# Gate rows of the expert blocks made on GpSimd instead of VectorE, in a two-layer diffusion step

## The reference

```python
    a = jax.nn.silu(hg) * hu * combine[..., None]
    y = jnp.einsum('nef,efd->nd', a, p["w_down"])
    ...
    x = x + g2 * _hier_moe(h2, p)      # once for the context, once for the latents
```

## Time and profile before

| | |
|---|---|
| time, median of 3 runs | 1197.59 us (1192.82 to 1198.98) |
| profiled execution: its own time, its span | 1193.6 us, 1191.8 us |
| TensorE clock granted, mean | 0.969 |
| busy: PE, DVE, ACT, POOL | 1068.1, 678.8, 433.7, 196.3 us |
| chain of waits: PE, DMA, DVE, POOL | 71%, 11%, 9%, 2% |
| mean DMA rate over the span | 224 GB/s |

### The profile page before, as it was taken

The page is one execution under the profiler, slowest core; times in us unless marked ns, Lnnn a source line. Parts: engine busy times, 40 slices in busy tenths (PEclk is TensorE's granted clock), DMA queues, the critical chain, the costliest instruction groups (busy, mean ns, idle before and its releaser), DMA issues.

```text
span 1191.8 us, 23434 instructions
## 1 busy us (share of the span) xinstructions
PE 1068.1 (90%) x9769; PEld 886.1 (74%) x9769; DVE 678.8 (57%) x1441; ACT 433.7 (36%) x935; POOL 196.3 (16%) x228
## 2 busy tenths in 40 slices
PE   3889999999999989999669999999999998999960
PEld 1567778889997668888447677888998876888850
DVE  1434466555466667766563336555446766666663
ACT  2332235652433413323242223655233342333321
POOL 0011140000021122221131112200001212222113
PEclk9999999999999999999889999999999999999985
DMA  9797989223337599999857998322243566999934
GB/s 316 238 242 206 230 276 348 71 77 107 107 105 261 199 350 360 371 359 379 286 180 213 240 232 251 94 71 71 76 141 102 213 226 220 339 363 372 378 114 176
DMA packets 136734, 267.00 MB, mean 224 GB/s; under 512 B 9989, under 2 KB 92069, under 8 KB 128432
## 3 DMA queue, kind: packets, MB, share of 16 engines
q1 hardware_dynamic: 118992, 219.13, 53.5%
q0 software_dynamic: 17024, 44.69, 13.3%
q10 hardware_dynamic: 608, 1.62, 0.4%
HBM read 248.71 MB, written 28.31 MB: 232 GB/s over the span
## 4 chain that ended last, share of the span: by engine, by line
PE 71%; DMA 11%; DVE 9%; issue 3%; ACT 3%; POOL 2%; SPq 1%; DVEq 0%; POOLq 0%; ACTq 0%
PE ps L938 16%; PE ps L809 16%; PE ps L1146 10%; PE ps L1058 6%; DMA ring<-in_w_down 5%; PE ps L1187 5%; PE ps L1073 5%; PE ps L690 3%; DMA ring<-in_ada_w 2%; DMA ring<-in_w_in 2%; PE ps L882 2%; PE ps L922 2%; PE ps L904 2%; PE ps L1136 1%; DMA arena<-scratch_xs,token_i 1%
## 5 line engine op out<-in xcount | busy, mean ns | idle before, releaser
L579 DVE TENSOR_TENSOR w_lo<-ring,w_hi 128x512 fp32r<-128x512 f32 x128 | 87.7, 690 | 162.1 <-ACT w_hi L568 162.0
L568 ACT ACTIVATE w_hi<-ring 128x512 fp32r<-128x512 f32 x128 | 80.3, 631 | 239.0 <-PE ps L809 142.0
L576 DVE TENSOR_TENSOR w_lo<-ring,w_hi 128x512 fp32r<-128x512 f32 x128 | 88.0, 689 | 109.9 <-ACT w_hi L566 109.9
L938 PE MATMUL ps<-h_hi,w_hi 128*128 128x384 f32 x384 | 133.8, 348 | 4.6 <-ACT arena L2175 4.6
L566 ACT ACTIVATE w_hi<-ring 128x512 fp32r<-128x512 f32 x128 | 80.4, 629 | 149.2 <-PE ps L938 103.8
L938 PE MATMUL ps<-h_hi,w_lo 128*128 128x384 f32 x384 | 128.8, 335 | 0.0
L938 PE MATMUL ps<-h_lo,w_hi 128*128 128x384 f32 x384 | 128.7, 335 | 0.0
L809 PE MATMUL ps<-w_hi,h_hi 128*128 128x512 f32 x288 | 117.0, 406 | 12.4 <-DVE w_lo L579 5.8
L809 PE MATMUL ps<-w_hi,h_lo 128*128 128x512 f32 x288 | 114.1, 396 | 0.0
L809 PE MATMUL ps<-w_lo,h_hi 128*128 128x512 f32 x288 | 114.1, 396 | 0.0
L1146 PEld LDWEIGHTS ps<-arena,ring 128*64 128x64 f32 x1920 | 80.2, 137 | 6.4 <-issue 6.3
(11 more groups left out here) (316 smaller groups left out, 2119.6 us busy)
## 6 DMA issues: line engine op xcount, KB each, us to landing
ring<-in_w_in SPq DMA_DIRECT2D x48, 1024.0 KB, 5.3
ring<-in_ada_w SPq DMA_DIRECT2D x44, 1024.0 KB, 10.2
ring<-in_w_down SPq DMA_DIRECT2D x18, 1024.0 KB, 17.0
ring<-in_w_up SPq DMA_DIRECT2D x16, 1024.0 KB, 13.2
ring<-in_w_gate SPq DMA_DIRECT2D x14, 1024.0 KB, 13.2
arena<-in_w_gate SPq DMA_DIRECT2D x10, 1024.0 KB, 9.2
scratch_ys<-x POOLq DMA_DIRECT2D x1, 9216.0 KB, 29.2
ring<-in_w_out SPq DMA_DIRECT2D x8, 1024.0 KB, 5.0
```

Source lines behind the costliest of these rows:

```text
L568: eng.activation(w_hi[:, q % 2], ring[:, slot, 2 * q:2 * q + 2, :], ACT.Copy).then_inc(whi_ready, 1)
L576: eng.tensor_tensor(gate_weights(w_lo, q), ring[:, SLOT[seg, l, c], k0:k0 + 4, j * P:(j + 1) * P], gate_weights(w_hi, q).bitcast(F32), ALU ...
L579: eng.tensor_tensor(w_lo[:, q % 2], ring[:, SLOT[seg, l, c], 2 * q:2 * q + 2, :], w_hi[:, q % 2].bitcast(F32), ALU.subtract).then_inc(wlo_ ...
L938: mm = pe.matmul(ps[:, bank, 0:TOK], gate_weights(wx, q)[:, kk, :], hx[:, k, :], start=(k == 0 and n == 0), stop=(k == KT - 1 and n == 2))
```

## The change

VectorE no longer makes gate rows for the 16 blocks. GpSimd makes them by two instructions for each block, a tensor_scalar and a tensor_tensor, with a wait of GpSimd for its own first one between them. The rows of blocks 0 and 1 are made before its loop, the row of block b+2 behind the store of block b (and the gather of block b+4). `output_copied(e)` waits for `gates_made`. In layer 0 GpSimd waits, ahead of its first gate row, until the next layer's modulation rows, which lie in the same tile, have been read (`mod_rows_ready`). A single block that overflows still gets its gate row on VectorE.

```diff
-                link(dve.tensor_tensor(gb[:, 0, :], gb[:, 0, :], gb[:, 1, :], ALU.subtract))
-                linked()
+                dve.tensor_tensor(gb[:, 0, :], gb[:, 0, :], gb[:, 1, :], ALU.subtract).then_inc(gate_rows, 1)
...
-                def output_copied(e, gate_made=False):
-                    if not gate_made:
-                        link(block_gate(e))
+                def output_copied(e):
+                    dve.wait_ge(gates_made, blocks(l, e) + 1)
...
                     down_low(e - 1)
-                    if e == N_EXP - 1:
-                        dve.wait_ge(y_second, l * N_EXP + e)
-                        link(block_gate(e - 1))
-                        link(block_gate(e))
                     activated(e)
...
+                def block_gate(b):
+
+                    step(pool.tensor_scalar(slot_gate[:, b % 2], gb[0:CAP, 0, :], slot_ctx[:, b:b + 1], 1.0, ALU.mult, ALU.mult))
+                    pool.tensor_tensor(slot_gate[:, b % 2], slot_gate[:, b % 2], gb[0:CAP, 1, :], ALU.add).then_inc(gates_made, 1)
+
                 pool.wait_ge(rows_ready, l + 1)
+                pool.wait_ge(gate_rows, l + 1)
+                if l + 1 < DEPTH:
+                    pool.wait_ge(mod_rows_ready, MODS.index((l + 1, 0)) + 1)
+                block_gate(0)
+                block_gate(1)
                 for b in range(N_EXP):
...
                         load_block(b + 4)
+                    if b + 2 < N_EXP:
+                        block_gate(b + 2)
```

More of the change, by code:

```diff
@@ L441, in build @@
         rows_ready = sem("rows_ready")
+        gate_rows = sem("gate_rows")
+        gates_made = sem("gates_made")
         xg_loaded = [sem(f"xg_loaded{i}") for i in range(4)]
@@ L1956, in _ @@
                         down_low(e, (0, 1))
-                    output_copied(e - 1, e == N_EXP - 1)
+                    output_copied(e - 1)
                     if e == 1 and l + 1 < DEPTH:
@@ L1960, in _ @@
                 down_low(N_EXP - 1, (2, 3))
-                output_copied(N_EXP - 1, True)
+                output_copied(N_EXP - 1)
                 dve.wait_ge(routed, l + 1)
```

## The result

| | before | after |
|---|---|---|
| median, 20 runs each | 1194.78 us (1190.28 to 1198.98) | 1198.06 us (1194.1 to 1204.57) |
| ratio to before, 95% | | 1.0033, 1.0017 to 1.0048 |
| profiled execution: its own time, its span | 1193.6, 1191.8 us | 1200.73, 1198.7 us |
| TensorE clock granted, mean | 0.969 | 0.963 |
| busy: PE, DVE, ACT, POOL | 1068.1, 678.8, 433.7, 196.3 us | 1075.6, 685.9, 434.8, 316.8 us |

What follows compares the result with a forecast made beforehand. Weight loads bound the expert stages, so what follows the last landing counts. End collisions of +1.2 us a layer gave 1197.6 + 2.4 = 1200.0 us, other terms 0; own range 1196 to 1203, 8 in 10 within 1192.5 to 1206.

Steps and rivals of the forecast that it cites:

- no change within 0.5%: Whole kernel: a time difference within 0.5% (6.0 us), neither slower nor faster by that; given 81%.
- the 5 us of queue ahead of every chunk hide that: Layer 0's expert stage: queued weight transfers cover the 2.7 us late gather; cost 0, or 2.7 us without cover.
- the late start of layer 0: Block 0's pair waits for the modulation rows' copy; outputs some 2.5 us later, TensorE's gathered rows 2.7 us late once.
- Rival 3: Layer 0's late start not hidden, or collisions inside the stage reach the weights: 2.7 plus 2.3 us, 1205.0; 14%.
- the collision at the end: End of each layer's expert stage: block 15's GpSimd pair and VectorE's `h_lo` take turns; +1.2 us a layer, +2.4.
- the gain on offer: End of each expert stage: without two gate rows, expert 15's activation (L1909) starts 1.54 us earlier in each layer.
- the gate rows inside the stage: Inside each expert stage: removing 14 gate rows a layer from VectorE, 17.9 us, is worth 0 by itself.
- the pair costs 3.6 us: GpSimd's tensor_scalar and tensor_tensor for one block, with the wait between: 1.2 + 0.1 + 2.26 = 3.6 us; ends 3.3 and 7.4.
- GpSimd's turn fits: Expert stage: GpSimd needs 6.6 us a turn with the pair, within TensorE's turn of 9.02 us.
- the output multiplication does not collide: L1895 on VectorE, one input in PSUM: collision with GpSimd taken as 0, up to 2.3 us once a turn otherwise.
- Rival 2: Expert stages: GpSimd sets the pace once a pair takes over 6.03 us; +9.1 us a layer, 1215.8; 8%.
- VectorE's busy time down by some 40 us: Sign expected in the profile after: VectorE's busy time falls by some 40 us, less the waits inside its instructions.

Runs made afterwards that it cites:

- r6: Kernel before, with only the gate rows of blocks 0 and 1 of layer 0 made on GpSimd, behind the modulation-rows wait; ratio 1.0041, +4.9 us.
- r1: Changed kernel with the gate rows in another tile, so GpSimd needs no wait for the modulation rows; ratio 0.9990 to the kernel before.
- r8: Kernel before, plus four GpSimd memsets of 96x1024 into an unread tile at each place where the changed kernel has its pair; ratio 1.0003.
- r2: Kernel before with no gate rows at all, every slot multiplied by the latent tokens' row; ratio 0.9976, 2.9 us less.
- r3: Kernel before with each layer's last two gate rows moved on VectorE, ahead of the low parts of experts 13 and 14; ratio 0.9982.
- r4: Kernel before, VectorE making all gate rows, plus GpSimd making the pairs into an unread tile without the modulation-rows wait; ratio 1.0079, +9.4 us.
- r5: Changed kernel with only block 1's pair moved on GpSimd, behind the store and gather of block 0; ratio 1.0016 to the kernel before.
- r7: r1 with the gate rows of blocks 14 and 15 back on VectorE, placed as in r3; ratio 0.9978 to the kernel before.

## Why the prediction was right in size and wrong in place

The forecast was +2.4 us; +3.9 was measured. Its range, and "no change within 0.5%", held. That is luck: all of the +2.4 was forecast for the ends of the layers, where no loss stands clear of the spread, and what was measured came from a step that the forecast set at 0. The forecast median was 1200.0 and 1198.06 was measured; its base, 1197.59 from three runs of the kernel before, lies 2.8 us above the 1194.78 of twenty.

- **Failed: "the 5 us of queue ahead of every chunk hide that"**, of the late start of layer 0. Set at 0, with 2.7 us if the cover were gone. It cost 4.5 us at the last landing; r6, the late start alone, costs 4.9 us, and r1, which takes it away, brings the ratio to 0.9990. Two errors are in the step. First its size. The tensor_tensor of block 1 was taken to go first, with the four `h_lo` behind it, and to be through by 457.6. It was the other way round: it took 5.01 us, the issue of the gather then took 2.67 us in place of 0.98, and TensorE was 5.2 us late, not 2.7. Second the cover: TensorE frees the slots for the next loads, and with the slower clock behind its wait SyncE's next load was 7.4 us late, more than the 4.7 us that the queue lasted by my own figure of 7.7 - 3.0. And it did not last that long: the DMA engines lost 4.6 us (4.1 + 0.45), so my estimate of what the queue covered is 7.4 - 4.6 = 2.8 us. Rival 3 named this mechanism and had 14%.
- **Partly right: the collision at the end, +1.2 us in each layer.** Layer 0: L1910 at 5.54 us behind the first `h_lo`, where 6.0 was forecast and 4.81 stood before, so +0.73. In the time it is not shown: from the last landing to the end of the outputs it takes 13.8 us in layer 0 and 12.6 in layer 1, and the traces in which VectorE makes these two gate rows as before (before, r6, r8) have 12.6 to 13.8. Layer 1: no collision. The pair came 2.2 us behind the start of `h_lo` there, since the turns of the two engines had shifted against each other. The forecast built on the pair being ready 0.5 us behind the first `h_lo` (1145.3 against 1144.78), at the end of a long sum, which could not tell that place within a microsecond.
- **Right, as far as it can be told: the gain on offer.** 2 x 1.54 = 3.1 us forecast; 2.9 us by r2 (0 to 5.6), and r3 brings L1909 forward by 1.44 us.
- **Right: the gate rows inside the stage are worth about 0** (r2 and r3 differ by 0.7 us, within their intervals), the pair costs 3.6 us (1.13 + 2.41 = 3.54 measured, without the wait between), GpSimd's turn fits, the output multiplication does not collide. Rival 2 fell: GpSimd idled 2.43 us ahead of the stores at 1058.61 and 1067.76, where it had been 6.03.
- **Wrong, harmless: VectorE's busy time down by some 40 us.** It rose by 7.1: the waits inside `w_lo` and `h_lo` ate it all. The forecast had allowed for "less the waits", and nothing hung on it.

The sum by what was measured: the last landing of layer 0 +4.5, and nothing else that stands clear of the spread between executions; measured 3.9, between 2.0 and 5.7 by the interval.

Of the Trainium skill, SBUF — State Buffer, section "SBUF: two separate sides", the rule of an exclusive lock between a VectorE operation with two SBUF inputs and a GpSimd operation that reads SBUF is borne out by w_lo's 1478 ns and r4's 3400 ns, by the PSUM-fed L1896 at 736 ns, and by r8's memsets, which read nothing. By that rule the one that starts first has the pair for its whole instruction. The traces agree in part. The tensor_tensor at 583.21 let one `h_lo` pass and held the next (583.59 to 586.47). But the one at 455.38 stood through four `h_lo` that by the profile began 0.25 us behind it, and GpSimd's spans in a profile are rough. So who goes first stays open; no run here orders the two on purpose.

## What to carry to other kernels

Before moving elementwise work off an engine that is not the bound, look for the few instances of it that stand behind the last landing. Moving just these into the same engine's idle time (r3) gave nearly the ratio of removing all 32 (0.9982 and 0.9976, with intervals that reach 1). The queue that receives the work has its own duties: here a gather stood behind it, behind the gather a slot of weights, and the cover that a deep queue gives must be compared with the whole delay at its end, not with the first link's. The tile in which a result is put brings the waits of its former user along, and one such wait outweighed every other effect of the change here.

## What the runs showed of the hardware that was not expected

- A GpSimd tensor_tensor took 5.01 us where its kind takes 2.36, as it waited for four VectorE instructions in a row (4.99 and 4.93 us in r6 and r5).
- Issues of indirect DMAs on GpSimd are stretched beside `h_lo`: 2.67 us for a gather in place of 0.98; in r7 a store's issue took 3.63 us, beside a gate row and four `h_lo`.
- GpSimd memsets of 96x1024 (958 ns) stretched no instruction of VectorE: `h_lo` took 677/681/693 ns, `w_lo` 357/358/361, the gate row 1273/1274/1277.
- The granted clock had fallen to 0.50 before TensorE's wait of 5.05 us ended (0.68 from 469 to 470 us, 0.50 from 470), stayed there while TensorE worked from 471.39 on, and was 0.91 from 476 to 477 us.
